# A convolutional feed-forward stage: ScalarE and VectorE work skewed by one item, PSUM released at its read

## The reference, cut to what matters

```python
h2 = rmsnorm(x, g2) * (1 + sc2) + sh2
def conv_ffn(h, prev, w_up, conv_w, conv_b, w_down):
    up = h @ w_up                                  # (T, 1024) @ (1024, 5632)
    z = jnp.concatenate([prev, up], axis=1)
    y = conv_b
    for j in range(3):                             # causal, per channel
        y = y + conv_w[j] * z[:, j:j + T]
    a, b = jnp.split(y, 2, axis=-1)
    return (jax.nn.silu(a) * b) @ w_down, z[:, -2:]
x = x + gt2 * f
```

## Time and profile before

| | |
|---|---|
| median of three runs | 1001.7 us |
| the profiled execution: its time | 1000.68 us |
| its span, first to last instruction | 998.8 us |
| TensorE busy (matmul / weight load) | 87% / 76% |
| VectorE, ScalarE, GpSimd busy | 50%, 36%, 34% |
| mean granted TensorE clock | 0.895 of full speed |
| chain that ended last, by engine | PE 52%, DVE 26%, ACT 13% |

### The profile page before, as it was taken

How to read it: one execution, slowest core, us unless ns; L and a number is a source line. 1 busy time by engine, 2 the same in 40 slices (tenths; PEclk the granted TensorE clock), 3 DMA queues, 4 the chain that set the end, 5 groups by cost and what they waited for, 6 DMA issues and landing times.

```text
span 998.8 us, 19158 instructions
## 1 busy us (share of the span) xinstructions
PE 871.2 (87%) x7555; PEld 762.3 (76%) x7555; DVE 499.2 (50%) x938; ACT 358.4 (36%) x684; POOL 338.3 (34%) x204
## 2 busy tenths in 40 slices
PE   4869999998997787777799699999899999998994
PEld 3668899995465545445599599988899999888994
DVE  0153365655459845554447655555521455655223
ACT  3442222224332234334332544444321344444222
POOL 0033564530004843223324033333344333333330
PEclk9579999997556559889999899999999999999997
DMA  9632878762048724411026122333222333222222
GB/s 350 242 127 87 265 252 266 254 228 56 2 119 321 251 40 119 125 55 54 2 72 239 43 80 101 106 106 107 88 92 85 106 107 106 85 85 80 77 73 85
DMA packets 72440, 128.29 MB, mean 128 GB/s; under 512 B 13653, under 2 KB 48157, under 8 KB 72097
## 3 DMA queue, kind: packets, MB, share of 16 engines
q1 hardware_dynamic: 65664, 109.65, 33.2%
q10 hardware_dynamic: 6656, 17.43, 5.0%
q0 software_dynamic: 32, 0.00, 0.0%
HBM read 121.39 MB, written 9.11 MB: 131 GB/s over the span
## 4 chain that ended last, share of the span: by engine, by line
PE 52%; DVE 26%; ACT 13%; issue 5%; ACTq 1%; POOL 1%; DMA 1%; SPq 1%; DVEq 0%
PE ps L675 29%; DVE arena L1726 5%; ACT wR L1027 4%; ACT arena L1271 3%; DVE arena L1731 3%; DVE arena L1730 3%; ACT arena L1269 2%; PE ps L945 2%; PE ps L658 2%; PE ps L843 2%; PE ps L858 2%; PE ps L895 2%; PE ps L927 2%; DVE arena L1738 1%; PE ps L732 1%
## 5 line engine op out<-in xcount | busy, mean ns | idle before, releaser
L675 PE MATMUL ps<-hR,wR 128*128 128x260 f32 x3504 | 440.8, 286 | 31.1 <-DVE arena L1726 14.6
L675 PEld LDWEIGHTS ps<-hR,wR 128*128 128x128 f32 x3504 | 428.8, 190 | 42.1 <-DVE arena L1726 20.9
L629 POOL TENSOR_TENSOR wR<-raw,wR 128x1024 fp32r<-128x1024 f32 x95 | 228.0, 2400 | 356.1 <-ACT wR L1027 356.1
L1027 ACT ACTIVATE wR<-raw 128x1024 fp32r<-128x1024 f32 x95 | 99.7, 1050 | 104.1 <-PE ps L675 100.5
L675 PE MATMUL ps<-fR,wR 128*128 128x260 f32 x1056 | 129.8, 285 | 6.9 <-DVE fR L1740 5.0
L675 PEld LDWEIGHTS ps<-fR,wR 128*128 128x128 f32 x1056 | 128.6, 190 | 8.1 <-DVE fR L1740 5.4
L1726 DVE COPY arena<-arena 128x2 f32<-128x2 f32 x44 | 48.8, 1109 | 108.6 <-ACT arena L1271 108.6
L623 POOL TENSOR_SCALAR arena<-arena,fac 128x128 f32<-128x128 f32 (+3 forms) x32 | 40.9, 1277 | 92.0 <-DVE fac L1651 92.0
L566 POOL TENSOR_TENSOR arena<-arena,par 128x1024 f32<-128x1024 f32 x16 | 33.5, 2093 | 88.5 <-DMA arena<-cache_keys 88.5
L1222 ACT ACTIVATE arena<-ps,nmx 128x128 f32<-128x128 f32 (+3 forms) x64 | 33.2, 523 | 81.7 <-DVE nmx L1642 55.0
L1338 DVE TENSOR_REDUCE arena<-arena 128x64 f32<-128x1024 f32 x16 | 19.5, 1219 | 83.2 <-POOL arena L566 83.2
(11 more groups left out here) (339 smaller groups left out, 1034.5 us busy)
## 6 DMA issues: line engine op xcount, KB each, us to landing
raw<-weights SPq DMA_DIRECT2D x95, 512.0 KB, 3.7
arena<-cache_keys SPq DMA_DIRECT2D x128, 192.0 KB, 3.2
arena<-weights SPq DMA_DIRECT2D x24, 512.0 KB, 10.5
arena<-cache_values SPq DMA_DIRECT2D x128, 64.0 KB, 1.8
arena<-weights ACTq DMA_DIRECT2D x12, 512.0 KB, 5.7
raw<-weights ACTq DMA_DIRECT2D x12, 512.0 KB, 4.8
x<-xT SPq DMA_DIRECT2D x8, 260.0 KB, 6.3
out_y<-x SPq DMA_DIRECT2D x8, 260.0 KB, 2.2
```

Source lines behind the costliest of these rows:

```text
L629: nc.gpsimd.tensor_tensor(wR[:, i % 2, 1, :, :], raw[:, g % RAW, :, :], wR[:, i % 2, 0, :, :].bitcast(F32), ALU.subtract).then_inc(lo_read ...
L675: last = mm(ps[:, a + half, 0:TH], wR[:, i % 2, wp, k, :], src[:, hp, j, half * TH:(half + 1) * TH], start=(j == 0 and q == 0), stop=(j == ...
L1027: A(wR[:, i % 2, 0, :, :], raw[:, g % RAW, :, :], ACT.Identity).then_inc(hi_ready, 1)
```

## The change

The whole diff, but for the declaration of `y_used`, which goes:

```diff
+def residuals(m):
+    return sum(kind != "up" for kind, _, _ in PART2[:m + 1])
+
+def last_up(j):
+    return j % FH == FH - 1
...
             for m, (kind, t, _) in enumerate(PART2):
                 if m >= 2:
-                    pe.wait_ge(evac_dve, m - 1)
+                    old, ot, _ = PART2[m - 2]
+                    if old == "up":
+                        pe.wait_ge(y_ready, 2 * (2 * (ot % FC) + ot // FC) + 1)
+                    else:
+                        pe.wait_ge(evac_dve, residuals(m - 2))
                 product(len(PART1) + m)
...
+            def f_high(j):
+                act.wait_ge(f_ready, j + 1)
+                if j == FH:
+                    act.wait_ge(evac_dve, residuals(PART2_AT["down0", KD - 1]))
+                A(fR[:, 0, j % FH, :], yab[:, 1, :], ACT.Identity).then_inc(f_hi, 1)
...
-                while nhi < len(SPLIT) and SPLIT[nhi - 2] < CHUNK0[n + 1] // KD:
+                tail = kind == "up" and t >= FC and last_up(t % FC)
+                while not tail and nhi < len(SPLIT) and SPLIT[nhi - 2] < CHUNK0[n + 1] // KD:
                     hi(nhi)
                     nhi += 1
...
-                    if v >= 2:
-                        act.wait_ge(y_used, v - 1)
+                    if b == 0 and j:
+                        act.wait_ge(silu_in, j)
+                    if b == 1 and j:
+                        act.wait_ge(f_lo, j)
                     if v == 0:
                         act.wait_ge(zero_done, 1)
-                    link(A(zb[:, b, 2:T + 2]..., ps[:, 2 * (n % 2):2 * (n % 2) + 2, 0:TH], ACT.Identity))
+                    A(zb[:, b, 2:T + 2]..., ps[:, ...], ACT.Identity).then_inc(y_ready, 1)
+                    act.wait_ge(y_ready, 2 * v + 1)
                     A(yab[:, b, :], zb[:, b, 2:T + 2], ACT.Identity, bias=..., scale=...).then_inc(y_ready, 1)
-                    if b == 0:
+                    while tail and nhi < len(SPLIT) and SPLIT[nhi - 2] < CHUNK0[n + 1] // KD:
+                        hi(nhi)
+                        nhi += 1
+                    if b == 0 and j and not last_up(j - 1):
+                        f_high(j - 1)
+                    if b == 1:
                         act.wait_ge(silu_in, j + 1)
                         if j:
                             act.wait_ge(f_ready, j)
                         A(sil[:, :], yab[:, 0, :], ACT.Silu).then_inc(silu_out, 1)
-                    else:
-                        act.wait_ge(f_ready, j + 1)
-                        if j == FH:
-                            act.wait_ge(evac_dve, PART2_AT["down0", KD - 1] + 1)
-                        A(fR[:, 0, j % FH, :], yab[:, 1, :], ACT.Identity).then_inc(f_hi, 1)
+                        if tail:
+                            f_high(j)
...
+            def f_low(j):
+                dve.wait_ge(f_hi, j + 1)
+                V.tensor_tensor(fR[:, 1, j % FH, :], yab[:, 1, :], fR[:, 0, j % FH, :].bitcast(F32), ALU.subtract).then_inc(f_lo, 1)
...
-                    dve.wait_ge(y_ready, v + 1)
-                    nc.vector.tensor_copy(ffo_p[:, t, :], z[:, S:S + 2]).then_inc(evac_dve, 1)
+                    dve.wait_ge(y_ready, 2 * v + 2)
+                    V.tensor_copy(ffo_p[:, t, :], z[:, S:S + 2])
...
                     if b == 0:
                         last.then_inc(silu_in, 1)
-                        dve.wait_ge(silu_out, j + 1)
-                        dve.sem_inc(y_used, 1)
+                        if j and not last_up(j - 1):
+                            f_low(j - 1)
                     else:
                         link(last)
+                        dve.wait_ge(silu_out, j + 1)
                         V.tensor_tensor(y, sil[:, :], y, ALU.mult).then_inc(f_ready, 1)
-                        dve.wait_ge(f_hi, j + 1)
-                        V.tensor_tensor(fR[:, 1, j % FH, :], y, fR[:, 0, j % FH, :].bitcast(F32), ALU.subtract).then_inc(f_lo, 1)
-                        dve.wait_ge(f_lo, j + 1)
-                        dve.sem_inc(y_used, 1)
+                        if last_up(j):
+                            f_low(j)
```

More of the change, by code:

```diff
@@ L315, in trunk_kernel @@
         f_ready, f_hi, f_lo = sem("f_ready"), sem("f_hi"), sem("f_lo")
-        y_used, zero_done = sem("y_used"), sem("zero_done")
+        zero_done = sem("zero_done")
         table_landed = sem("table_landed")
@@ L1264, in _ @@
                         act.dma_start(o_wv[:, v // 4 - 1], winV[:, v // 4 - 1]).then_inc(end_out, 16)
-                    if v >= 2:
-                        act.wait_ge(y_used, v - 1)
+                    if b == 0 and j:
+                        act.wait_ge(silu_in, j)
+                    if b == 1 and j:
+                        act.wait_ge(f_lo, j)
                     if v == 0:
                         act.wait_ge(zero_done, 1)
-                    link(A(zb[:, b, 2:T + 2].rearrange("p (a n) -> p a n", a=2), ps[:, 2 * (n % 2):2 * (n % 2) + 2, 0:TH],
-                           ACT.Identity))
+                    A(zb[:, b, 2:T + 2].rearrange("p (a n) -> p a n", a=2), ps[:, 2 * (n % 2):2 * (n % 2) + 2, 0:TH],
+                      ACT.Identity).then_inc(y_ready, 1)
+                    act.wait_ge(y_ready, 2 * v + 1)
                     A(yab[:, b, :], zb[:, b, 2:T + 2], ACT.Identity, bias=par_("conv_b", t, t + 1),
                       scale=par_("conv_w", 3 * t + 2, 3 * t + 3)).then_inc(y_ready, 1)
-                    if b == 0:
+                    while tail and nhi < len(SPLIT) and SPLIT[nhi - 2] < CHUNK0[n + 1] // KD:
[4 more added lines that the diff above has]
+                    if b == 1:
                         act.wait_ge(silu_in, j + 1)
```

## The result

The changed kernel takes 973.9 us in the median (973.0 to 982.0, 4 runs) against 1001.8 us (1000.7 to 1003.0, 4 runs) before; ratio 0.9725, 95% interval 0.9677 to 0.9774. 973.4 us were forecast. The profiled execution takes 973.88 us, its span is 972.0 us.

The account below looks back on a forecast made before the run. No engine was full; ScalarE and VectorE, waiting for each other, cost 1.5 us a pair. Savings 25.3 + 2.0 + 1.0 = 28.3 us from 1000.7 give 972.4, median 1.0 above: 973.4 us, range 968.5 to 980.

Parts of the forecast that it names:

- Bound and skew: Up stretches: ScalarE and VectorE, in line for each other, pace the pair; skewed, items take 5.76 us, saving 25.3 us.
- The narrow new wait: Up items b: the PSUM copy waits for VectorE's remainder `f_lo` of item a, with 0.4 us to spare.
- Both halves of the skew: Up items: SiLU and the result's rounding with its remainder each move one item later, so ScalarE waits for no same-item taps.
- Tails: Start of each down, chunks 8 and 10: TensorE idles 2.0 us instead of 3.0, saving 2 us together.
- H + 8.75: Last up item of a half: VectorE's chain ends 8.75 us after H, with GpSimd's 2.39 us in it.
- Clock: Behind the second tail: less idling makes the clock's fall less likely, saving 1.0 of 1.7 us.
- Port loop: Up stretches: VectorE and GpSimd exclude each other, a pair takes 12.1 instead of 11.52 us; 984 us, chance 0.08.
- Slower by the clock: Up stretches: the granted clock falls to 0.5 under unbroken TensorE load; 1037 us, chance 0.04.

Follow-up runs that it names:

- e1: The kernel before with the release alone: TensorE released by ScalarE's copy out of PSUM, order of work as before; ratio to before 0.9974.
- e2: The changed kernel with PSUM released by VectorE's two-column copy again, so the skew alone; 973.1 us.
- e7: The kernel before, but from the third up slot on GpSimd subtracts only half of each slot; order and waits as before; 973.7 us.
- e3: The changed kernel with only SiLU moved by one item; rounding and remainder of the result stay in item b; 975.7 us.
- e4: The changed kernel with only rounding and remainder of the result moved; SiLU stays in item a behind its own taps; 972.7 us.
- e5: The changed kernel with `hi` in front of the PSUM copy in the last item of a half too; 977.2 us.
- e11: The kernel before with the release, SiLU one item later and `hi` in front of the PSUM copy in every item; 972.2 us.
- e8: The changed kernel with two more unused VectorE instructions of 0.75 us in every up item; 1026.0 us.
- e6: The changed kernel with one more unused VectorE instruction of 0.75 us in every up item; 975.0 us.
- e9: The changed kernel with two more unused VectorE instructions per up item and, from the third up slot on, GpSimd's subtraction halved; 976.3 us.
- e10: The changed kernel with only SiLU moved and two more unused VectorE instructions per up item; one execution, up stretches 134.5 and 147.3 us.

## Why the prediction was right, step by step

- *Bound and skew.* 25.3 us forecast for the `up` stretches, 11.8 + 13.2 = 25.0 measured. The narrow new wait had 0.5 us to spare (L1738 ends at 642.22, the PSUM copy starts at 642.74) where 0.4 was forecast. That weights and copy were late together is shown by e1, that the skew alone brings the gain by e2. What the step left out is a part of why the pair was too long; e7 shows that without GpSimd's hold on the copy there would have been no loss. The prediction had seen that hold only as a reason for the copy's length. (ScalarE, said to be busy a little more than half of the time, was so for 46%; nothing hangs on it.)
- *Both halves of the skew* were taken as needed. e3 and e4 show that one is.
- *Tails.* 1.0 us saved each was forecast, 1.5 measured. I had TensorE idle 2.0 us; it idles 0.33 + 1.20. VectorE's chain ended at 707.83, where the forecast's H + 8.75 (H = 699.46) is 708.2. The forecast put GpSimd's whole 2.39 us into the chain; the held tap lost 2.0. The way was right, the size 0.5 us off in each half.
- *Clock.* 1.0 us forecast; the fall behind the second tail is gone and `down1` is 1.5 us shorter, nearly the whole 1.7 that was the upper bound. At the end it cost 0.8 us back: the clock falls to 1.2 GHz (half of full) before the last four norm products instead of during and behind them, and they take 2.10 us instead of 1.27. Before and after:

```profile
986.59 0.70 PE L646 MATMUL ps<-rstd,con 128*128 128x260 f32 x2 [2.79 <-DVE rstd L1307]
987.13 0.73 PE L647 MATMUL ps<-rstd,con 128*128 128x260 f32 x2
```
```profile
958.97 1.23 PE L657 MATMUL ps<-rstd,con 128*128 128x260 f32 x2 [2.78 <-DVE rstd L1336]
960.00 1.07 PE L658 MATMUL ps<-rstd,con 128*128 128x260 f32 x2
```

  Why it falls sooner stays open: e7, which has no wait in the tails, has the long products too, e5 and e11 the short ones.
- *Not foreseen* were the 0.8 us at the end and 1.9 us more ahead of the change, where the code is the same in all kernels and even the faster traces spread from 581.8 to 584.8 us. Term by term the profiled execution saved 25.0 + 3.0 + 1.5 - 1.9 - 0.8 = 26.8 us where 28.3 were forecast. The median fits to 0.5 us because it stood 1.0 us above the profiled execution before the change and 0.05 us after it. The pace of the `up` stretches was foreseen; that closeness is luck.
- *Port loop*, the rival at 984 us: it didn't come, but e8 shows that it exists, at 14.1 us a pair instead of 12.1 + 4 x 0.67 = 14.8 worked out the same way; with the 2.1 us that a held tap loses in e8 in place of 2.39 it would be 14.2. The changed kernel stands one VectorE instruction of 0.75 us from its edge.
- *Slower by the clock*: the grant was 1.00 through both `up` stretches.

## What to carry to other kernels

When two engines wait for each other in turn, one move of one step by one item may be enough; try each alone before both. A wait in the profile names the last of what came together, so ask what would be late next. Look for a tiny instruction with a long duration that ends with another engine's: here 0.94 us of exclusion per item, in a serial chain, turned an order that would have kept TensorE's pace into one that lost 1.5 us a pair, and the skew hides it only up to a sharp limit.

## What the hardware showed that was not expected

Ahead of the change, in an attention stage, one program has two courses about 7 us apart. The third `up` item starts at 582 to 585 us in the traces of before, the changed kernel, e1, e2, e4, e6, e8 and e11, and at 589 to 591 us in e3, e5, e7, e9 and e10. The code there is the same in all. Two windows of 10 us, first of the kernel before, then of e5:

```profile
405.00:415.00 10.00, 7.58 (x50) 4.18 (x48) 6.32 (x15) 3.44 (x10) 2.56 (x2) 0.83 0.44 128
415.00:425.00 10.00, 7.92 (x108) 5.41 (x104) 5.37 (x16) 5.40 (x15) 4.25 (x3) 1.00 0.39 114
```
```profile
405.00:415.00 10.00, 9.70 (x70) 4.93 (x60) 3.59 (x9) 1.93 (x6) 1.08 (x1) 0.52 0.41 117
415.00:425.00 10.00, 8.71 (x37) 4.42 (x38) 3.83 (x10) 3.66 (x10) 2.94 (x2) 0.50 0.37 103
```

The granted clock stays at its lower level there in e5 where it rose in the kernel before. All traces divide the same way: over 405 to 425 us the grant is 0.50 to 0.54 in the five late ones and 0.83 to 1.00 in the eight others. What decides between the two courses stays open. A gain of 1 or 2 us can't be measured by whole runs over such a stage; between two marks of the trace the `up` stretches repeat within 0.1 us.
